# Nine pairs instead of eight by seven block products in the first down projection, with the rotary angles two to a row

## The reference: what is computed

```python
def swiglu(x, w_gate, w_up, w_down):
    return (jax.nn.silu(x @ w_gate) * (x @ w_up)) @ w_down
...
        x = layer_norm(DN_ALPHA * x + h, ln_g[layer, 0], ln_b[layer, 0])
        x = layer_norm(DN_ALPHA * x + swiglu(x, ffn_w_gate[layer], ffn_w_up[layer], ffn_w_down[layer]),
                       ln_g[layer, 1], ln_b[layer, 1])
```

```python
    ang = positions.astype(jnp.float32)[..., None] * inv_freq
    cos = jnp.cos(ang)[:, :, None, :]
    sin = jnp.sin(ang)[:, :, None, :]
```

## Time and profile before

| | |
|---|---|
| median of 3 runs | 1346.6 us (1346.03 to 1347.04) |
| profiled execution | 1347.21 us, of which its span 1345.2 us |
| PE busy | 1331.1 us (99% of the span), 8007 matmuls |
| DVE, ACT, POOL busy | 969.1, 664.3, 408.8 us |
| granted TensorE clock, mean | 0.996 |
| DMA | 203.49 MB, mean 151 GB/s |

### The profile page before, as it was taken

The page is one execution under the profiler, slowest core; times in us unless marked ns, Lnnn a source line. Parts: engine busy times, 40 slices in busy tenths (PEclk is TensorE's granted clock), DMA queues, the critical chain, the costliest instruction groups (busy, mean ns, idle before and its releaser), DMA issues.

```text
span 1345.2 us, 20872 instructions
## 1 busy us (share of the span) xinstructions
PE 1331.1 (99%) x8007; PEld 1185.9 (88%) x8007; DVE 969.1 (72%) x1299; ACT 664.3 (49%) x1027; POOL 408.8 (30%) x250
## 2 busy tenths in 40 slices
PE   8999999999999999999999999999999999999997
PEld 7887899999988889888888888888889999999885
DVE  3998698888899856777433767634249888889977
ACT  4465655555566563233423343423355555555566
POOL 5798600000020044555444544344252000000002
PEclk9999999999999999999999999999999999999999
DMA  9977524334398626776466777454122334335553
GB/s 272 298 223 175 133 67 119 100 94 118 103 269 250 199 63 196 189 188 165 136 173 162 199 169 176 97 172 135 52 63 82 94 102 117 94 104 201 199 172 130
DMA packets 208172, 203.49 MB, mean 151 GB/s; under 512 B 11397, under 2 KB 164761, under 8 KB 207800
## 3 DMA queue, kind: packets, MB, share of 16 engines
q1 hardware_dynamic: 188104, 173.37, 42.8%
q0 software_dynamic: 13376, 24.91, 10.6%
q10 hardware_dynamic: 6624, 4.29, 1.3%
HBM read 198.30 MB, written 54.05 MB: 188 GB/s over the span
## 4 chain that ended last, share of the span: by engine, by line
PE 97%; ACT 1%; DVE 1%; DMA 1%; issue 0%; SPq 0%; DVEq 0%; ACTq 0%
PE pq L1202 10%; PE pq L1201 10%; PE pq L1199 10%; PE pq L874 9%; PE pq L876 9%; PE pq L875 9%; PE pq L896 8%; PE pq L898 7%; PE pq L897 7%; PE pq L1384 3%; PE pq L1383 3%; PE pq L1385 3%; PE pq L1362 1%; PE pq L1321 1%; PE pq L1334 1%; PE pq L1355 1%
## 5 line engine op out<-in xcount | busy, mean ns | idle before, releaser
L746 POOL TENSOR_TENSOR w_lo<-stage,w_hi 128x1024 fp32r<-128x1024 f32 x110 | 274.6, 2500 | 358.3 <-ACT w_hi L1456 358.2
L1456 ACT ACTIVATE w_hi<-stage 128x1024 fp32r<-128x1024 f32 (+1 forms) x186 | 192.3, 1049 | 167.6 <-PE pq L898 78.7
L874 PE MATMUL pq<-xt_hi,w_hi 128*128 128x512 f32 (+1 forms) x624 | 228.4, 366 | 0.5 <-DVE xt_lo L1965 0.4
L876 PE MATMUL pq<-xt_hi,w_lo 128*128 128x512 f32 (+1 forms) x624 | 225.2, 361 | 0.0
L875 PE MATMUL pq<-xt_lo,w_hi 128*128 128x512 f32 (+1 forms) x624 | 225.1, 361 | 0.0
L1201 PE MATMUL pq<-xt_lo,w_hi 128*128 128x256 f32 x632 | 178.9, 283 | 0.0
L1202 PE MATMUL pq<-xt_hi,w_lo 128*128 128x256 f32 x632 | 178.9, 283 | 0.0
L1199 PE MATMUL pq<-xt_hi,w_hi 128*128 128x256 f32 x632 | 178.8, 283 | 0.0
L874 PEld LDWEIGHTS pq<-xt_hi,w_hi 128*128 128x128 f32 x624 | 117.9, 189 | 19.5 <-DVE xt_lo L1965 1.2
L876 PEld LDWEIGHTS pq<-xt_hi,w_lo 128*128 128x128 f32 x624 | 117.8, 189 | 18.0
L1199 PE MATMUL pq<-xs_hi,w_hi 128*128 128x256 f32 x472 | 133.6, 283 | 0.0
(11 more groups left out here) (283 smaller groups left out, 2965.8 us busy)
## 6 DMA issues: line engine op xcount, KB each, us to landing
stage<-in_od_w_qkv_dram SPq DMA_DIRECT2D x72, 512.0 KB, 4.1
stage<-t_rows SPq DMA_DIRECT2D x46, 512.0 KB, 3.5
stage<-in_ffn_w_gate_dram SPq DMA_DIRECT2D x44, 512.0 KB, 5.0
stage<-in_ffn_w_up_dram SPq DMA_DIRECT2D x44, 512.0 KB, 3.9
t_rows<-in_ffn_w_down_dram SPq DMA_DIRECT2D x38, 512.0 KB, 7.2
stage<-in_ffn_w_down_dram SPq DMA_DIRECT2D x25, 512.0 KB, 4.1
t_rows<-in_ffn_w_down_dram POOLq DMA_DIRECT2D x19, 512.0 KB, 8.2
t_rows<-in_ffn_w_down_dram POOLq DMA_DIRECT2D x38, 256.0 KB, 6.2
```

The source lines that it names most:

```text
L746: pool.tensor_tensor(w_lo[slab % RING][:, :], w_stage[slab % RING][:, :], w_hi[slab % RING][:, :].bitcast(F32), ALU.subtract).then_inc(w_l ...
L874: pe.matmul(o, hi[:, k, :], x_hi, start=(k == 0), stop=False)
L876: last = pe.matmul(o, lo[:, k, :], x_hi, start=False, stop=(k == KD - 1))
L1456: act.activation(w_hi[slab % RING][:, 0:width], w_stage[slab % RING][:, 0:width], ACT.Copy).then_inc(w_hi_ready, 1)
```

## The change

Layer 0 gets a ninth pair. Its layout becomes 18 slabs of pairs, 2 front rows (18, 19), 5 slabs of fourth sums (20 to 24, the last of half width), 7 plain rows (25 to 31) and 4 whole rows (32 to 35): 36 slabs instead of 34. SP makes a ninth copy behind slab 19, POOL four more sums, and the gates of POOL's last sums are set closer. The four angle parts now stand two beside slab 32 and two beside slab 33, where they stood one each beside slabs 28 to 31.

```diff
-PAIRS = (8, KF // 2)
+PAIRS = (9, KF // 2)
...
-COPY_BEHIND = (8, 9, 10, 11, 12, 14, 15, 17)
+COPY_BEHIND = (8, 9, 10, 11, 12, 14, 15, 17, 19)
...
-LATER_SUMS = ((THREE, 4), (THREE, 5), (BOTH, 6), (OWN, 6), (BOTH, 7), (OWN, 7), (THREE, 6), (THREE, 7),
+LATER_SUMS = ((THREE, 4), (THREE, 5), (BOTH, 6), (OWN, 6), (BOTH, 7), (OWN, 7), (THREE, 6), (BOTH, 8), (OWN, 8), (THREE, 7), (THREE, 8),
               *((FOUR, j) for j in range(PAIRS[0])))
...
-                    pool.wait_ge(w_hi_ready, plain(S_DOWN0 + n - 2) + 1)
+                    pool.wait_ge(w_hi_ready, plain(S_DOWN0 + n - 2 - max(n - 11, 0) // 2) + 1)
...
                             low_row(slab)
-                            if whole_slabs <= slab < whole_slabs + 4:
-                                rotary_angles(slab - whole_slabs)
+                            if whole_slabs <= slab < whole_slabs + 2:
+                                rotary_angles(2 * (slab - whole_slabs))
+                                rotary_angles(2 * (slab - whole_slabs) + 1)
```

## The result

| | median of its runs, us | range | profiled execution | its span |
|---|---|---|---|---|
| before | 1346.6 | 1345.9 to 1347.6 (6 runs) | 1347.2 | 1345.2 |
| after | 1352.9 | 1352.4 to 1355.0 (6 runs) | 1352.8 | 1350.8 |

The ratio is 1.0051, with a 95% interval of 1.0041 to 1.0062: the change costs some 6 us. The forecast was 1352.1 us, in a range of 1349.6 to 1354.4.

A forecast was written before the change was run, and what follows sets the result against it. PE, busy 99% of the span, was taken as the bound. Matmuls -1.4, wait +5.2, fourth sums +0.3 and clock +1.4 gave +5.5 us on the median 1346.6: 1352.1 us, range 1349.6 to 1354.4.

The forecast's parts named there:

- The matmuls, -1.4 us: On PE in the changed stage: 474 matmuls instead of 480, six fewer at 0.2273 us, 1.4 us gained.
- The wait, 5.2 us: Before the last three whole rows: PE waits 5.2 us for slab 35's row, behind the angle parts and ACT's tables.
- The clock, +1.4 us: Behind PE's wait for the last rows: idleness lowers PE's granted clock, costing 1.4 us.
- Rival (a): The wait before the last rows is there but the clock stays up: +4.1 us, 1350.7 us; chance 0.25.
- a mean clock unchanged at 0.996: Sign over the whole execution that the clock had not fallen, pointing to Rival (a).
- The fourth sums, +0.3 us: At slab 20: the last fourth sum lands at 433.0, and the slab reaches DVE late, costing 0.3 us.
- I expect them to keep up over one more pair: In the pairs: slab loads keep PE's pace beside the ninth pair's added sums, costing nothing.
- Rival (b): Fourth sums or the pairs' slabs also late: up to 3.8 us more, 1352.1 to 1355.9 us; chance 0.10.
- Rival (c): Before the last three whole rows: angles stay hidden, only the matmuls count, 1345.2 us; chance 0.11.

The follow-up runs named there:

- e3_eight_late: Kernel before, eight pairs, with angle parts 0 and 1 moved beside slab 31 and 2 and 3 beside slab 32: 1351.0 us, ratio 1.0026.
- e1_spread: Changed kernel with its four angle parts moved to one each beside slabs 28, 30, 31 and 32: 1346.8 us, ratio 0.9996.
- e4_eight_two: Kernel before, eight pairs, with two angle parts beside slab 28 and two beside slab 29: 1346.4 us, ratio 1.0000.
- after_again: Changed kernel run once more with no edit, against runs of the kernel before: 1354.0 us, ratio 1.0054.
- e12_three_fours: On top of e10_second_tables_last, third sum of pair 7 put ahead of pair 8's second, pair 8's third behind the first fourth sum: 1351.7 us, ratio 1.0033.
- e10_second_tables_last: Changed kernel with angle parts beside slabs 26, 28, 30 and 32 and ACT's tables behind its last row: 1346.8 us, ratio 1.0004.
- e5_no_angles: Changed kernel without the angles' arithmetic: parts 0 and 1 empty, parts 2 and 3 one instruction each: 1346.8 us, ratio 1.0001.
- e2_tables_last: Changed kernel with ACT's sine and cosine tables moved behind the w_hi of the last slab: 1352.7 us, ratio 1.0043.
- e9_every_second: Changed kernel with one angle part each beside slabs 26, 28, 30 and 32: 1347.1 us, ratio 1.0001.
- e6b_busy_six: Changed kernel with 6 fp32 products of zeros added ahead of PE's wait for the last three whole rows: 1352.9 us, ratio 1.0053.
- e6_busy_wait: Changed kernel with 12 fp32 products of zeros added ahead of PE's wait for the last three whole rows: 1357.0 us, ratio 1.0073.
- e7_two_at_end: Changed kernel with only slabs 34 and 35 finished tile by tile, slab 33 in PE's plain loop: 1351.5 us, ratio 1.0040.

## Why the prediction was right, and where not

**The matmuls, -1.4 us: right.** 8001 matmuls after, 8007 before, and the last column of the table shows the 1.3 us by itself.

**The wait, 5.2 us: right in place and mechanism, measured 5.5.** The times read close to the forecast: first part at 465.32 (465.69), w_hi of slab 35 at 477.99 (478.40), row ended at 480.22 + 0.68 = 480.90 (481.32), PE ready at 475.83 (476.16). That they are within 0.45 us is partly luck, since the stage began 1.26 us earlier here than before (382.78 against 384.04). Counted from the stage's start all four came 0.84 to 0.93 us later than forecast, about what the pairs waited more (below). Between them they keep the forecast's distances to 0.1 us: from the first part to PE's asking are 10.51 us (10.5), and the chain is 15.58 us long (15.6). The missing 0.3 is a small term of its own: PE's first matmul began 0.47 us after DVE's row had ended (as in e3_eight_late), and the sum had counted that as 0. e1_spread, e3_eight_late and e4_eight_two show that the place of the parts is cause enough, with and without the ninth pair.

**The clock, +1.4 us: right in kind, measured 1.7 in this execution, at the upper end of its bounds,** 2.3 in after_again. The trace of before showed a low stretch of 3.3 us; here it was 6.8 us, half of it inside the wait, so that the part under work was about the 3.4 us of the bound. In after_again 4.9 us of it lay in the work, past that bound. Rival (a), a clock that stays up, is out. The one ground that this term had in the trace was weaker than it looked: the case of the earlier trace rows, "a wait of 2.0 us and transposes did that", is not to be had in most executions (last section). And the sign set for it, a mean clock unchanged at 0.996, could not tell: the profiled executions of the changed kernel have 0.995 and 0.996, since the mean of before holds the low stretch at the start.

**The fourth sums, +0.3 us: the time was right, the cost 0.** SP's timeline shows the loads of the slabs of fourth sums, the first sent when the last sum had landed, against 423.91 of before:

```profile
432.16 6.43 SPq L631 DMA_DIRECT2D stage<-t_rows  x5
```

That is 49.4 us into the stage, for a forecast of 433.0 - 384.04 = 49.0, and PE had no wait at slab 20.

**"I expect them to keep up over one more pair", 0 us: this step was wrong.** It took the rate of 404 to 412 as free of charge since PE had not waited there before, and did not follow which load waits for which sum. SP's waits after the change show it (waited for: us in total, times, longest); in the view of before there is no such row:

```profile
SPq L631 <- DMA t_rows<-in_ffn_w_down_dram: 2.7, 1, 2.7
```

That is a pair's load held back by its third sum. None of the three kernels with eight pairs has it, every one with nine has. The waits of PE to 442 are 0.58 to 0.84 us in the three executions with eight pairs, and, but for e1_spread, more with nine. Leaving out e12_three_fours and the two kernels with products added, the eight are 1.66, 1.81, 0.72, 1.32, 1.63, 2.43, 3.35 and 0.98, 1.7 on the mean: 1.0 us more than the 0.72 of eight pairs. From slab 8 on, PE's waits grow with SP's: 0.3 us in e1_spread, where such sums held SP for 0.5 us, 1.0 in after (2.7), 1.7 in e10_second_tables_last (3.2) and 2.6 in e5_no_angles (3.8). The kernels with eight pairs have 0.3 there. These kernels do not differ from each other up to slab 26, so the spread from 0.72 to 3.35 is one of executions, and each kernel has but one profiled; a third of the 1.0 us lies ahead of slab 8 and is not explained. On the mean it eats most of the 1.4 us, and four kernels of nine pairs without the large gap time as before, with ratios of 0.9996 to 1.0004. Rival (b) named late slabs of the pairs, but set its test at the fourth sums.

**The sum.** -1.3 + 5.5 + 1.7 + 0.8 (1.66 - 0.84) = 6.7 us, against 6.85 of the stage. The medians differ by 6.3, the profiled executions by 5.6, since the stage began 1.26 us earlier in that of after. Forecast were 5.5: the clock, the row's 0.3 and the pairs' 0.8 are what was short, and 0.3 for the fourth sums was too much.

**Rival (c), the angles hidden,** needed the last row by 476.16. It came at 480.90, with PE ready at 475.83. With the tables out of the way (e2_tables_last) the two rows behind part 3 end at 480.72, with PE ready at 476.9.

## What to carry to other kernels

A fill-in task on an idle-looking engine is hidden by distance, not by share: measure from its start to the last item made behind it, and set that against how far ahead of the consumer it starts. DVE was at 72% in both kernels; moving the first angle part up by four rows and the last by one (e1_spread) was worth some 7 us. When a change shortens the consumer's side, as replacing whole rows by products did here, every fill-in has to move up with it, and so has whatever a second engine queues behind the fill-in (ACT's tables). And a stream of transfers that has never made anyone wait may still have nothing to spare: where loads and sums share the engines, ask what one unit more would delay, and weigh that against the few matmuls that it saves.

## What the runs showed of the hardware

**The clock's fall depends on the wait.** After gaps of 0.8 and 2.8 us (e1_spread, e3_eight_late) the granted clock stayed at 1.00. After gaps of 4.3 and 4.0 us (e2_tables_last, e12_three_fours) it fell for 3.4 us, after PE had already resumed at full speed. After 5.5 us it was low for 6.8 us, from within the wait. The stretch in e12_three_fours:

```profile
432.00:436.00 4.00, 4.00 (x13) 3.16 (x12) 3.26 (x4) 1.70 (x4) 0.00 (x0) 0.60 0.48 172
```

So a wait of 4.3 to 5.5 us cost another 1.7 to 2.3 us that lies behind it (e2_tables_last, after, after_again).

At the start of the span the same kernel may or may not pay. In five of the fourteen profiled executions (before, e2_tables_last, e3_eight_late, e4_eight_two, e9_every_second) the clock was low for some 3.4 us from about 10.8 us on, as in the earlier trace rows; in the nine others it stayed at 1.00. PE's work just ahead was much the same: these two rows are of after_again, where PE was busy for 1.16 us and the clock stayed up, against 1.23 us and a fall in before:

```profile
7.30:10.70 3.40, 1.16 (x9) 0.85 (x8) 1.60 (x4) 2.46 (x5) 1.51 (x1) 1.00 1.05 380
10.80:14.10 3.30, 3.30 (x29) 3.30 (x30) 2.46 (x4) 2.43 (x4) 1.27 (x2) 1.00 1.20 294
```

The five are those in which the down projection begins at 384.0 us or later, some 1.5 us behind the others. So a fall seen in one execution's trace is not a property of the kernel, and two profiled spans can differ by this much with nothing changed.

**Matmul prices.** At the lower clock (after) a 512-column product started every 0.427 us, at the upper every 0.2273. A plain fp32 product of 512 columns (e6b_busy_six) went as two instructions of 0.43 us each, at the upper clock.

**A short DVE instruction can take five times as long.** L2215 (32x512) took 2.58 us after the change and 0.47 before. In the seven profiled executions where it took 2.6 us (after, after_again, e2_tables_last, e3_eight_late, e6_busy_wait, e6b_busy_six, e7_two_at_end) it began 0.2 to 0.4 us after POOL's split of a 128x1024 slab and ended 0.3 us after it; in the seven others it was over before POOL's split began, and took 0.47. POOL's timeline after the change:

```profile
480.65 2.47 POOL L746 TENSOR_TENSOR w_lo<-stage,w_hi 128x1024 fp32r<-128x1024 f32 x1 [65.09 <-ACT w_hi L1456]
```

DVE's ran from 480.82 to 483.40. The Trainium skill (SBUF — State Buffer, SBUF: two separate sides) says that DVE, in those of its instructions that need the pair, and GpSimd share a pair of ports that whichever starts first holds for its whole instruction, the other being blocked; this agrees. Here it cost nothing: DVE's next instruction waited for PE until 487.47.
